# Coefficient buffer laid out by query part, and first work of the last stage reordered

## The reference

```
q = (hb @ w_q).reshape(C, PEER_HEADS, 2, PEER_DK_HALF)
s = jnp.einsum('thpd,hpnd->thpn', q, sub_keys)
sv, si = lax.top_k(s, PEER_TOPK)
...                     # the 16 best of 256 pairs, for each of 8 heads
g = jax.nn.softmax(fv, axis=-1).reshape(C, PEER_HEADS * PEER_TOPK)
u = u_tab[eidx]
a = jax.nn.gelu(jnp.einsum('ted,td->te', u, hb), approximate=False)
coef = (g * a)
vv = v_tab[eidx]
return jnp.einsum('te,ted->td', coef, vv)
```

## Time and profile before

| | us |
|---|---|
| median of 3 runs | 3193.61 |
| lowest, highest | 3193.11, 3198.58 |
| the profiled execution's own time | 3193.11 |
| its span | 3191.3 |
| PE busy | 3084.2 (97%) |
| DVE busy | 2011.6 (63%) |
| ACT busy | 1271.5 (40%) |
| POOL busy | 759.9 (24%) |

### The profile page before, as it was taken

One profiled execution on the slowest core, in us unless ns is written; L12 is line 12 of the kernel. 1 busy time (PEld: TensorE's weight loads), 2 busy tenths in 40 slices (PEclk: granted clock), 3 DMA queues, 4 the chain that ended last, 5 costly groups with the idle time before them and its releaser, 6 DMA issues.

```text
span 3191.3 us, 42667 instructions
## 1 busy us (share of the span) xinstructions
PE 3084.2 (97%) x16801; PEld 2688.5 (84%) x16801; DVE 2011.6 (63%) x3594; ACT 1271.5 (40%) x2173; POOL 759.9 (24%) x515
## 2 busy tenths in 40 slices
PE   8999999989999999999999999999999999999999
PEld 6769989878888888888877778999999897888887
DVE  5676565653332464333257755888988876787878
ACT  6364443433322334332234632435445453333332
POOL 1000110100000020000001200676776755443332
PEclk9999999999999999999999999999999999999999
DMA  4303221233332323332322022578889889999997
GB/s 128 106 28 100 60 67 54 73 113 93 99 99 93 119 85 97 97 99 94 91 84 79 1 68 79 183 269 292 300 272 331 277 315 365 363 353 366 346 359 265
DMA packets 233352, 539.36 MB, mean 169 GB/s; under 512 B 24817, under 2 KB 91633, under 8 KB 231105
## 3 DMA queue, kind: packets, MB, share of 16 engines
q1 hardware_dynamic: 195712, 400.27, 37.8%
q0 software_dynamic: 37440, 136.36, 11.7%
HBM read 484.10 MB, written 52.46 MB: 168 GB/s over the span
## 4 chain that ended last, share of the span: by engine, by line
PE 81%; DVE 8%; DMA 4%; POOL 3%; ACT 2%; issue 1%; SPq 0%; DVEq 0%; ACTq 0%
PE bank L382 22%; PE bank L385 15%; PE bank L2817 14%; PE bank L2385 11%; PE bank L2545 3%; PE bank L1109 2%; DMA eu<-in_peer_u 2%; PE bank L1119 2%; POOL etl L2373 2%; PE bank L1058 2%; PE bank L1070 2%; DMA gl<-acts 1%; PE bank L505 1%; PE bank L797 1%; POOL taken L2410 1%
## 5 line engine op out<-in xcount | busy, mean ns | idle before, releaser
L332 DVE TENSOR_TENSOR wl<-raw,wh 128x1024 fp32r<-128x1024 f32 (+2 forms) x241 | 297.0, 1235 | 643.2 <-ACT wh L317 643.1
L317 ACT CAST wh<-raw 128x1024 fp32r<-128x1024 f32 (+2 forms) x241 | 249.7, 1038 | 656.9 <-PE bank L382 366.3
L2373 POOL TENSOR_TENSOR etl<-eu,eth 128x1024 fp32r<-128x1024 f32 x128 | 316.3, 2473 | 396.8 <-ACT eth L2369 395.9
L2385 PE MATMUL bank<-peerhh,eth 128*128 128x384 f32 x1024 | 349.1, 341 | 16.5 <-POOL etl L2373 14.3
L2385 PE MATMUL bank<-peerhh,etl 128*128 128x384 f32 x1024 | 343.8, 336 | 0.0
L2385 PE MATMUL bank<-peerhl,eth 128*128 128x384 f32 x1024 | 343.6, 336 | 0.0
L2817 PE MATMUL bank<-vsh,coefh 128*128 128x512 f32 x768 | 299.7, 390 | 5.8 <-DVE coefl L2881 5.8
L2817 PE MATMUL bank<-vsl,coefh 128*128 128x512 f32 x768 | 299.3, 390 | 0.0
L2817 PE MATMUL bank<-vsh,coefl 128*128 128x512 f32 x768 | 299.3, 390 | 0.0
L2410 POOL DMA_INDIRECT taken<-in_peer_v,gb x128 | 196.3, 1533 | 315.1 <-DVE y_row L2430 303.3
L2369 ACT CAST eth<-eu 128x1024 fp32r<-128x1024 f32 x128 | 135.5, 1059 | 213.0 <-DMA eu<-in_peer_u 212.9
(11 more groups left out here) (571 smaller groups left out, 7181.0 us busy)
## 6 DMA issues: line engine op xcount, KB each, us to landing
eu<-in_peer_u SPq DMA_DIRECT2D x128, 512.0 KB, 4.5
vb<-in_peer_v SPq DMA_DIRECT2D x128, 512.0 KB, 5.6
raw<-in_ada_w SPq DMA_DIRECT2D x48, 512.0 KB, 3.9
acts<-eg SPq DMA_DIRECT2D x128, 192.0 KB, 4.1
coefs<-stage SPq DMA_DIRECT2D x24, 1024.0 KB, 8.9
gd<-coefs SPq DMA_DIRECT2D x16, 1536.0 KB, 10.4
gl<-acts SPq DMA_DIRECT2D x128, 192.0 KB, 7.5
raw<-in_ffn_w_gate SPq DMA_DIRECT2D x44, 512.0 KB, 3.6
```

The lines of the kernel that those rows point to most:

```text
L317: act.copy(parts_of(c)[0], raw_of(c)).then_inc(*up("w rounded", c))
L332: dve.tensor_tensor(lo, raw_of(c), hi.bitcast(F32), ALU.subtract).then_inc(*up("w split", c))
L2373: pool.tensor_tensor(Et[j % 3][1], Eu[j % 2], Et[j % 3][0].bitcast(F32), ALU.subtract).then_inc(*up("u split", j))
L2385: t = pe.matmul(b, tb[un][:, k * 128:(k + 1) * 128], peer_h[hn][:, k, 1:4, :], start=k == 0 and i == 0, stop=k == 7 and i == 2)
```

## The change

It has three parts.

1. The DRAM tensor `coefs` has another layout. Before, it was [16 blocks of 8 j][128 partitions][12 parts][256]: a write of half a part left 8 runs of 1 KB per partition, and the load of a block read 12 KB per partition in one run. After, it is [12 parts][128 partitions][4096]: a write is one run of 8 KB per partition, and a load reads 12 runs of 1 KB per partition, one from each part, which lie 2 MiB apart.
2. On ACT, the Gelu of the last unit (j=127) comes right behind `vsh` of j=0, and not behind `coefh` of j=1. On SP, the store of that unit comes ahead of the loads of j=3 and 4.
3. On DVE, 7 of the 128 sums come at the head of the expert phase: 4 before `vsl` of j=0, and 3 between it and the first `prod`. The other 121 are spread over the steps.

```diff
-    Gd = nc.dram_tensor("coefs", [16, 128, 12, 256], F32, kind="Internal").ap()
+    Gd = nc.dram_tensor("coefs", [12, 128, 128 * 32], F32, kind="Internal").ap()
...
-                    sp.dma_start(Gd[8 * half:8 * half + 8, :, tt * 4 - 4 + part, :].rearrange("g i x -> i g x"),
-                                 stage[part % 2][:, 64 * half:64 * half + 64, :].rearrange(
-                                     "p (g j) t -> p g (j t)", j=8)).then_inc(
+                    sp.dma_start(Gd[tt * 4 - 4 + part][:, 2048 * half:2048 * half + 2048],
+                                 stage[part % 2][:, 64 * half:64 * half + 64, :].rearrange("p j t -> p (j t)")).then_inc(
...
+    FIRST_SUMS = 4, 7
...
-                sp.dma_start(Gb[j // 8 % 2], Gd[j // 8].rearrange("i h x -> i (h x)")).then_inc(
+                sp.dma_start(Gb[j // 8 % 2].rearrange("p (h x) -> p h x", h=12),
+                             Gd.rearrange("h i x -> i h x")[:, :, 32 * j:32 * j + 256]).then_inc(
...
-        load(3)
-        load(4)
         sp_store(sp, on_sp, NJ - 1)
-        for j in range(5, NJ):
+        for j in range(3, NJ):
             load(j)
...
         units.until(NJ - 1)
+        v_part(0)
+        units()
         for j in range(NJ):
-            v_part(j)
+            if j:
+                v_part(j)
             coef_part(j)
-            if j == 1:
-                units()
...
+        sums(FIRST_SUMS[0])
         v_rest(0)
+        sums(FIRST_SUMS[1])
         prod(0)
...
-            sums(min(128, 128 * (j + 1) // (NJ - 1)))
+            sums(min(128, FIRST_SUMS[1] + (128 - FIRST_SUMS[1]) * (j + 1) // (NJ - 1)))
```

## The result

The changed kernel takes 3212.5 us (median; 3210.5 to 3217.3), the kernel before 3194.0 us on the same chip: ratio 1.0063, 95% interval 1.0047 to 1.0080. By these medians, of five runs each, it is 18.5 us slower. On record are 16 runs of the changed kernel (3208.7 to 3225.8, median 3213.7), and by the ratio it is 20 us. 3198 was predicted, and the range ended at 3207. The profiled execution took 3211.23 us, its span is 3209.4. PE is busy for 3087.8 us (96%).

The account below looks back on a forecast made before the run. The prediction took PE to bound the expert phase. Its terms, +8.5 - 0.7 - 3.5 + 0 = +4.3 us on 3193.11, gave 3197.4, or 3198 as a median; the 8-in-10 range was 3187 to 3207.

Parts of the forecast that it names:

- The passage: Between routing and expert phase: sums wait for rows, PE starts 8.5 us later; 0.7 us of later PE idle goes.
- The writes: Routing phase: coefficient writes in larger packets shorten PE's waits for `eu` loads behind them, gaining 3.5 us.
- The loads: Expert phase: `gd` loads in 1 KB packets cost PE 0, hidden by room on the DMA engines.
- The size of the load: Expert phase: each `gd` load takes all engines 4.4 us instead of 3.7, +0.7 us.
- Rival C: Expert phase: 1 KB runs make DMA engines the bound, from 86 ns per packet; 3206 at twice 46 ns; chance 0.14.
- Rivals A and B: A: the passage costs nothing, 3189.4, chance 0.14. B: writes caused the routing stalls, nearly all 12.6 us goes, 3186.4, chance 0.14.

Follow-up runs that it names:

- e2: Parts 2 and 3 alone, with the old layout of `coefs`, against the kernel before: 3203.9 us, ratio 1.0035.
- e9: Part 1 alone, each `gd` block after the first loaded in four pieces behind `gl` of four successive steps: 3195.0 us, ratio 1.0001 to the kernel before.
- e10: The kernel before with its `gd` loads, after the first block, in the same four pieces as e9: 3195.7 us, ratio 1.0003.
- e12: e9 with the reordered head of e11: 3190.0 us, ratio 0.9991 to the kernel before.
- e11: e10 with first `gd` block loaded ahead of v of j=0, and first `coefl` ahead of the second product: 3190.4 us, ratio 0.9993 to the kernel before.
- e5: Part 1 alone, `gd` loads issued by ACT on its own queue, eight steps ahead except the first two blocks: 3205.8 us, ratio 1.0034 to the kernel before.
- e13: The changed kernel with each `gd` block after the first loaded in four pieces, as in e9: 3202.0 us, ratio 1.0025 to the kernel before.
- e14: Part 1 alone, each `gd` block after the first loaded whole but issued five steps ahead of its use: 3216.9 us, ratio 1.0071 to the kernel before.
- e6: The kernel before with `gd` loads issued by ACT on its own queue, as in e5: 3199.3 us, ratio 1.0013.
- e1: Part 1 alone, the new layout of `coefs` with the old passage, against the kernel before: 3215.7 us, ratio 1.0064.
- e3: The changed kernel without the seven sums at the head, so parts 1 and 2: 3216.1 us, ratio 1.0075 to the kernel before.
- e4: The changed kernel with 4 KB of padding behind each part in `coefs`: 3276.6 us, ratio 1.0270 to the kernel before.
- e7: Part 1 alone with 127 of the 128 gathers of v rows and their sums left out: 3188.5 us, one execution.

## Why the prediction was wrong

- **The passage** (+8.5 - 0.7): the mechanism was right, the size a little small. e2 alone cost 9.8 us, and in the changed kernel PE started 8.8 us later. That this is so near 8.5, and the end of the seventh sum (2668.8) so near the predicted 2668.5, is in part luck. The takes began 2.8 us earlier than in before (2647.71 against 2650.54), and the seventh went out at 2659.59 (2661.3 predicted); but the second row took 9.0 us to land against 8.1, and the seventh 7.9 where 6.0 was assumed. PE's idle time grew by 11.6 us in the changed kernel and by 10.3 in e2, where 8 to 10 were forecast.
- **The writes** (-3.5): too large. Their landing fell from 8.9 to 7.1 us, but the engines' own time for a write fell from 3.1 us (1 KB packets at 49 ns, 2100 to 2640) to 2.8 (8 KB packets at 351 ns), by 0.3 us and not 0.5. The three stalls fell from 12.6 to 11.0 us. PE's last activation matmul ended at 2656.6 in the mean of ten traces with the new layout and at 2657.2 in that of six with the old, with a spread of 2652.2 to 2659.5. A gain of 0.7 us can't be told from none; e9 with e10 and e12 with e11 show none in time.
- **The loads** (0): this is the step that failed: "I cost it at 0. What hides it is the room of the DMA engines". The room was there (e5, e9 and e13 have the same packets and PE never waits), and a packet did cost 49 ns and not 86. But the room is a mean over 200 us, and the stall is one of latency: a `gl` stands behind the burst in the same queue (e14), with a short lead on its use. SP issues the loads of j once `vsl` of j-3 is done, and from there DVE has one sum and two steps to go. When DVE runs free, a step takes it 3.27 us (the `y_row` rows of the chain above), and the lead is 7.3 us in the changed kernel; at PE's pace, 4.08 us a step, it is 8.8 (e9). The `gl` behind the burst lands after 13.9.
- **The threshold.** DVE can make up 4.08 - 3.27 = 0.81 us per step, 6.5 us in the 8 steps of a block. Its waits for `gl` in 2730 to 3180, over the 13.8 blocks of that stretch, are 3.8 us per block in before, 3.0 in e2 and e6, 2.7 in e5, and PE never waits; 7.2 in the changed kernel, 7.5 in e1, 7.1 in e14, 6.8 in e3 and 9.1 in e4, and PE waits in all five. This could have been read before: 52.2 us of waits in 22 places, 3.8 of 6.5 spent, and only 2.7 us per block to spare. The late `gl` came 2.2 us later in the changed kernel (13.9 against 11.7), and DVE, no longer held up elsewhere in the block, was ready for it 1.1 us sooner (7.3 against 8.4): together 3.3 us, more than was left.
- **The size of the load** was too small as well: +0.7 us predicted, +2.2 without rows, +3.6 beside them.
- **Rival C** had the right place and sign but the wrong mechanism: the engines never were the bound, and the condition it named was not met. **Rivals A and B**: the passage did cost, and the writes were not the whole cause of the stalls, of which 11.0 of 12.6 us stayed.
- **The sum.** 9.8 for parts 2 and 3 and 20.8 for the burst (e1 less e9) would be 30.6 us; 18.5 were measured. Once DVE and `gl` set the pace, PE's late start is hidden in part, and the seven sums already done leave DVE 8.3 us less to do. Both stay argued. For the first e3 speaks, which starts PE 4.0 us later than e1 and takes the same time; for the second there is only the difference of e3 to the changed kernel, 3.5 us with overlapping intervals.

## What to carry to other kernels

A transfer's cost is not only its time on the DMA engines but what stands behind it in its queue. Before making a bulk load finer-grained, find the small urgent load issued behind it, compare its landing with the lead at which it is issued, and read how much slack per period its consumer has used already. The mean room of the DMA engines does not answer this; here the load in four pieces behind the urgent ones cost nothing that can be measured (e9, 1.0001). And a list of work moved ahead of a critical result must have its data: seven sums fitted DVE's idle time, but their rows did not arrive in it.

## Not expected of the hardware

- A load of 1536 runs of 1 KB held the next issue on SP for 2.88 us in the median of the changed kernel (0.61 to 7.33), where one of 128 runs of 12 KB let it pass in 0.38 (at most 0.54, before). Without the rows of v the hold was 0.76 (e7).
- POOL's indirect DMA instructions in 2730 to 3180 took a median of 2.37 us in the changed kernel and 1.01 in before, with nothing changed in them. The 1 KB packets beside them are not the reason: e5, e9 and e13 have these too, and 1.01. The long ones stand where DVE runs without a pause; the take at 2922.97, while DVE waited, took 0.94.
- The pad of 4 KB per 2 MiB made each 1 KB packet 61 ns instead of 49.5, and the kernel 64 us slower.
- A `gd` load on a third queue spread over 19.2 us (e5) instead of 10.3 (e1) in the new layout; in the old one it took 6.3 (e6), against 6.7.
